# A two-block transformer on one core: block 1's norms leave their inputs undivided and multiply every accumulator by the inverse root

## The reference

```python
def rms_norm(x, g):
    xf = x.astype(jnp.float32)
    y = xf * lax.rsqrt(jnp.mean(xf * xf, axis=-1, keepdims=True) + EPS)
    return (y * g.astype(jnp.float32)).astype(x.dtype)

for l in range(DEPTH):                      # DEPTH = 2
    h = rms_norm(x, attn_norm_g[l])
    proj = h @ w_in[l]                      # 28 tiles of 128 outputs
    rq, rk, rv, rg, dq, dk, dv = jnp.split(proj, split_at, axis=-1)
    ...                                     # retention, gated by silu(rg); differential attention
    x = x + jnp.concatenate([ret, da], axis=-1) @ w_out[l]
    h = rms_norm(x, ffn_norm_g[l])
    x = x + (jax.nn.silu(h @ w_gate[l]) * (h @ w_up[l])) @ w_down[l]
```

## Time and profile before

| what | value |
|---|---|
| runs | 3076.81, 3080.22, 3081.91 us (median 3080.22) |
| the profiled execution | 3072.54 us, of which its span 3070.8 |
| granted TensorE clock, mean of the span | 0.988 of 2.4 GHz |
| busy: TensorE, VectorE, ScalarE, GpSimd | 97%, 52%, 37%, 34% |

### The profile page before, as it was taken

The page is one execution under the profiler, slowest core; times in us unless marked ns, Lnnn a source line. Parts: engine busy times, 40 slices in busy tenths (PEclk is TensorE's granted clock), DMA queues, the critical chain, the costliest instruction groups (busy, mean ns, idle before and its releaser), DMA issues.

```text
span 3070.8 us, 46525 instructions
## 1 busy us (share of the span) xinstructions
PE 2980.6 (97%) x16904; PEld 2394.7 (78%) x16904; DVE 1592.3 (52%) x2527; ACT 1144.7 (37%) x1735; POOL 1053.4 (34%) x458
## 2 busy tenths in 40 slices
PE   8999999999999999999999999999999899999999
PEld 6866787887857788877886788888888667878887
DVE  5357654556357544554316746541552347567372
ACT  4264441223274542232227733321232327543232
POOL 3433444443433444442220033222223330244443
PEclk9999999999999999999999999999999999999999
DMA  4421343433411343431121111121221120122223
GB/s 165 139 105 37 128 148 126 146 131 105 168 55 56 129 143 131 145 122 48 55 65 39 49 49 55 61 70 54 67 67 64 55 63 2 38 86 95 91 97 101
DMA packets 78028, 272.74 MB, mean 89 GB/s; under 512 B 8160, under 2 KB 15328, under 8 KB 77792
## 3 DMA queue, kind: packets, MB, share of 16 engines
q1 hardware_dynamic: 76256, 267.09, 26.6%
q10 hardware_dynamic: 1664, 4.18, 0.4%
HBM read 269.14 MB, written 2.10 MB: 88 GB/s over the span
## 4 chain that ended last, share of the span: by engine, by line
PE 57%; issue 26%; POOL 8%; DVE 5%; ACT 2%; POOLq 0%; DMA 0%; ACTq 0%; DVEq 0%
PE ps L653 43%; POOL w_lo L552 7%; PE ps L691 4%; PE ps L1038 1%; PE ps L731 1%; PE ps L1020 1%; PE ps L773 1%; DVE s_s L2042 1%; PE ps L881 1%; PE ps L870 1%; DVE s_s L2032 1%; PE ps L905 1%; PE ps L862 1%; DVE h_lo L1671 1%; PE ps L894 1%
## 5 line engine op out<-in xcount | busy, mean ns | idle before, releaser
L552 POOL TENSOR_TENSOR w_lo<-w_raw,w_hi 128x1024 fp32r<-128x1024 f32 (+1 forms) x364 | 945.2, 2597 | 1521.9 <-ACT w_hi L1156 1521.9
L653 PE MATMUL ps<-h_hi,w_hi 128*128 128x512 f32 (+1 forms) x2832 | 953.8, 371 | 4.6 <-DVE proj L1702 2.3
L653 PE MATMUL ps<-h_lo,w_hi 128*128 128x512 f32 (+1 forms) x2832 | 945.3, 368 | 0.0
L653 PE MATMUL ps<-h_hi,w_lo 128*128 128x512 f32 (+1 forms) x2832 | 945.2, 368 | 0.0
L1156 ACT ACTIVATE w_hi<-w_raw 128x1024 fp32r<-128x1024 f32 (+1 forms) x364 | 406.3, 1116 | 1346.7 <-PE ps L653 1225.5
L653 PEld LDWEIGHTS ps<-h_hi,w_hi 128*128 128x128 f32 x2832 | 490.6, 188 | 111.5 <-issue 12.7
L653 PEld LDWEIGHTS ps<-h_hi,w_lo 128*128 128x128 f32 x2832 | 490.2, 188 | 90.9
L653 PEld LDWEIGHTS ps<-h_lo,w_hi 128*128 128x128 f32 x2832 | 490.5, 188 | 88.6
L1816 DVE TENSOR_SCALAR conv_y<-u_pad,small 128x770 f32<-128x770 f32 (+1 forms) x88 | 176.3, 2004 | 192.2 <-ACT u_pad L1338 192.0
L1769 DVE SCALAR_TENSOR_TENSOR xT<-ps,mod,xT 128x512 f32 (+1 forms) x72 | 45.4, 659 | 306.7 <-PE ps L653 260.0
L1604 DVE CUSTOM_DVE_ANT_0 mod_junk<-mod_w,silu_c 128x1024 f32<-128x1024 f32 x96 | 140.7, 1465 | 118.7 <-DMA mod_w<-w_mod_dram 116.8
(11 more groups left out here) (213 smaller groups left out, 3702.6 us busy)
## 6 DMA issues: line engine op xcount, KB each, us to landing
mod_w<-w_mod_dram SPq DMA_DIRECT2D x96, 512.0 KB, 3.5
w_raw<-w_gu_dram SPq DMA_DIRECT2D x88, 512.0 KB, 3.3
w_raw<-w_down_dram SPq DMA_DIRECT2D x64, 704.0 KB, 4.0
w_raw<-w_up_dram SPq DMA_DIRECT2D x88, 512.0 KB, 3.3
w_raw<-w_in_dram SPq DMA_DIRECT2D x56, 512.0 KB, 3.4
w_raw<-na_qkv_dram SPq DMA_DIRECT2D x24, 512.0 KB, 3.3
w_raw<-w_out_dram SPq DMA_DIRECT2D x16, 512.0 KB, 3.4
n_bias<-rpb_dram SPq DMA_DIRECT2D x24, 256.0 KB, 3.0
```

What stands on the lines that cost most here:

```text
L552: pool.tensor_tensor(w_lo[par][:, 0:cols], w_raw[par][:, 0:cols], w_hi[par][:, 0:cols].bitcast(F32), ALU.subtract).then_inc(w_lo_ready, 1)
L653: last = pe.matmul(acc[par][:, to:to + n], w[par][:, k * P:k * P + P], r[:, k, frm:frm + n], start=begin, stop=end)
```

## The change

Block 1's norms are of a new kind, `late`. Its inputs are not divided by the root: `h_hi` is ScalarE's copy of `xT` times the gain (a column of `small`), and `h_lo` is VectorE's `xT * gain - h_hi`, for all 8 tiles (GpSimd makes none). The root is worked out while the first pair behind the norm runs: `pack_norm` stands in `fresh_pair` after its fourth step (after the tenth at the start of the kernel), `spread_norm` after the eleventh (fourteenth), a step being three matmuls. `fresh_pair` now runs the first unit whole and then the second (`alternate(8)`). VectorE copies the spread inverse roots into a tile in SBUF, `rb` [128, 512], and every accumulator of w_in and of gate and up is multiplied by it on VectorE:

- the 16 plain units and the 4 of the gate's silu per layer, which ScalarE copied before (L1273), are now VectorE's (`take_proj`); the silu is then ScalarE's, in place in SBUF
- the normed units were VectorE's copy (L1702) and are its product now
- in `glu` VectorE makes `glu_g = acc[0] * rb`, ScalarE `silu(glu_g)` in place, VectorE `glu_g * rb`, and `glu_a = acc[1] * glu_g` as before. The modulation stands between the first and the second of these; before it stood ahead of all

At the end of a `resid` of block 1, ScalarE's work is written out (`late_end`): h_hi 0, the last square, h_hi 1 and 2, w_hi of the second unit, h_hi 3 to 7, the root.

At the start of the kernel SP loads 32 columns of gains first; the first weights no longer wait for a part of x, the second unit's wait for the second quarter and `mod_w` for the last; ScalarE makes h_hi and w_hi as x comes and squares behind them; the set-up of small things, `condition` (the silu of c), and the first modulation come later.

Block 2's norms stay as they were.

```diff
-POOL_TILES = {"norm": (2, 4, 6), "mix": (0, 2, 5, 3, 6), "fin2": (0, 2, 4, 6)}
+POOL_TILES = {"late": (), "norm": (2, 4, 6), "mix": (0, 2, 5, 3, 6), "fin2": (0, 2, 4, 6)}
...
     def norm(block, layer, which, T):
-        add("norm", block=block, layer=layer, which=which, T=T)
+        add("late" if block == 1 else "norm", block=block, layer=layer, which=which, T=T)
...
         def _(sp):
-            sp.wait_ge(x_in[2], 16)
+            sp.dma_start(small[:, 0:GAINS], d["small"][:, 0:GAINS]).then_inc(gains_in, 16)
...
                         if not first:
                             sp.wait_ge(w_lo_ready, i * 2 + (u0 + par - 1))
+                        elif par:
+                            sp.wait_ge(x_in[1], 16)
...
                         if not first:
                             sp.wait_ge(mod_step, i * 2 + u0)
+                        else:
+                            sp.wait_ge(x_in[3], 16)
...
-                for par, k in LATE_LAST if hidden else alternate(6 if ph["T"] == S else 3):
+                order = LATE_LAST if hidden else alternate(KT if late else 6 if ph["T"] == S else 3)
+                for step, (par, k) in enumerate(order):
...
+                    if late and step == (9 if first else 3):
+                        pack_norm(ph["fresh"])
+                    if late and step == (13 if first else 10):
+                        spread_norm(ph["fresh"])
...
+                act.activation(n_sq[1][:, 0:S], xT[:, KT - 1, 0:S], ACT.Square).then_inc(n_sq_ready, 1)
+                hi_late(ph, 1)
+                hi_late(ph, 2)
+                split(1)
+                for k in range(3, KT):
+                    hi_late(ph, k)
+                root(ph)
+
+            def beginning(ph):
+
+                act.wait_ge(gains_in, 16)
+                for q in range(4):
+                    act.wait_ge(x_in[q], 16)
+                    hi_late(ph, 2 * q)
+                    hi_late(ph, 2 * q + 1)
+                    if q in (0, 2):
+                        hi_part(q // 2, 16, KT)
+                act.dma_start(lam_vec[:], d["lam"]).then_inc(loaded, 16)
+                act.dma_start(silu_c[:], d["c"]).then_inc(loaded, 16)
+                act.activation(stats[:, 20:21], eps1[:], ACT.Sqrt).then_inc(table_in, 1)
+                for k in range(KT):
+                    if k >= 2:
+                        act.wait_ge(n_added, k)
+                    act.activation(n_sq[k % 2][:, 0:S], xT[:, k, 0:S], ACT.Square).then_inc(n_sq_ready, 1)
+                root(ph)
...
+            def late(ph):
+
+                n0 = ph["norm0"]
...
+                def lo(k):
+                    dve.wait_ge(h_hi_ready, KT * ph["h0"] + k + 1)
+                    dve.scalar_tensor_tensor(out=h_lo[:, k, 0:S], in0=xT[:, k, 0:S],
+                                             scalar=col("g_" + ph["which"], KT * ph["layer"] + k),
+                                             in1=h_hi[:, k, 0:S].bitcast(F32), op0=ALU.mult, op1=ALU.subtract
+                                             ).then_inc(h_dve, 1)
...
+                for k in range(KT):
+                    lo(k)
+                    if k == 5 and n0:
+                        invert()
...
+                dve.wait_ge(n_cast, ph["chunk0"] + len(chunks(S)))
+                dve.tensor_copy(halves(row(rb[:])), spread_out(S)).then_inc(n_rb, 1)
...
+                def take(i, par):
+                    dve.wait_ge(mm_done, i * 2 + (ph["unit0"] + par + 1))
+                    dve.tensor_tensor(proj1[:, bass.ds(i * 2 + (ph["tile0"] + par), 1), :], row(acc[par][:, 0:S]), row(rb[:]),
+                                      ALU.mult).then_inc(acc_free, 1)
...
                 with dve.Fori(0, FH) as f:
+                    dve.wait_ge(mm_done, f * 2 + (ph["unit0"] + 1))
+                    dve.wait_ge(a_lo_ready, BEGUN + f + n0)
+                    dve.tensor_tensor(glu_g[:], acc[0][:, 0:S], rb[:], ALU.mult).then_inc(acc_free, 1)
                     modulation(f, ph["unit0"])
-                    dve.wait_ge(acc_free, f * 2 + (ph["unit0"] + 1))
+                    dve.wait_ge(glu_silu, f + (n0 + 1))
+                    dve.tensor_tensor(glu_g[:], glu_g[:], rb[:], ALU.mult).then_inc(glu_scaled, 1)
                     dve.wait_ge(mm_done, f * 2 + (ph["unit0"] + 2))
-                    dve.wait_ge(a_lo_ready, BEGUN + f + n0)
+                    dve.wait_ge(glu_scaled, f + (n0 + 1))
                     dve.tensor_tensor(glu_a[:], acc[1][:, 0:S], glu_g[:], ALU.mult).then_inc(acc_free, 1)
```

148 lines of the change are left out of this document (94 added, 54 removed).

## The result

The changed kernel takes 3086.91 us (median of 20 runs, 3080.98 to 3094.08) against 3079.29 us for the kernel before (median of 20). The ratio is 1.0027, with a 95% interval of 1.0019 to 1.0035, so it is slower by some 8 us. I had forecast 3.4 us faster: the sign is wrong. The measured median lies close to the 3087.8 us of rival 3, but by coincidence. That rival has the clock fall at all three norms and nothing gained at the start; what happened is mostly something else.

A forecast was written before the change was run, and what follows sets the result against it. TensorE, busy 97%, was taken as the bound. Gains of 12.1 us less 7.2 (gate/up loop) and 1.5 (clock) left 3.4 us; the profiled 3072.5 becomes 3069.1, plus 7.7 to the median gives 3076.8, range 3068 to 3087.

The forecast's parts named there:

- rival 3: Norms and start: clock falls again at all three norms, nothing gained at the start; 7.6 us slower, 3087.8; chance 0.15.
- Part 1: Norms ahead of the two gate/up stages: next pair starts 17.5 us after the last matmul's start; gains 3.7 and 3.3 us.
- Part 2: Norm ahead of layer 1's projections: TensorE gets the first accumulator 18.75 us after the last matmul's start; gain 1.6 us.
- Part 4: Gate/up loop: VectorE's second dot product holds up w_lo in first halves, 0.40 us a pair, 7.2 us lost; second halves nothing.
- rival 1: Gate/up loop hides its new work, so no pair is longer; 3069.6; chance 0.18.
- rival 2: Gate/up loop: VectorE reaches the second dot product late but still before w_lo; 0.86 us a pair, 3085.1; chance 0.10.
- rival 4: Norms: first pair is faster because h_lo 3 gets through ahead of w_lo; 2 us more at three norms, 3070.8; chance 0.07.
- Part 5: Block 1's projections and mix: VectorE's added accumulators and possible w_lo waits are covered, mix at most 0.3 us later; costed at nothing.
- Part 3: Start of the kernel: second pair starts at 32.2 instead of 35.71; gain 3.5 us, from 0 to 6 possible.
- The clock: First unit of three norms: 1.5 us lost to a lower TensorE clock.

The follow-up runs named there:

- split_last: Changed kernel with w_hi of the second unit moved behind h_hi 7 and the root, and the reciprocal behind h_lo 7; ratio to the kernel before 1.0007.

## Why the prediction was wrong, point by point

**What was right.** *Part 1*: the next pair at L+17.5 was forecast for two norms; measured 17.86, and 19.26 at the one where the clock fell. *Part 2*: 18.75 forecast, 20.04 measured with the clock down for 3.4 us; in the kernel with SP's other order, whose norms are the same, it is 18.54 without. *Part 4*: 0.40 us a pair and 7.2 in all were forecast, 0.43 and 7.7 measured, with w_lo, dot product and TensorE within 0.1 us of the times in the text, and nothing inside the second halves. Rivals 1, 2 and 4 fell with that. Here too the Trainium skill's rule of the one that comes later and fully blocks ("SBUF — State Buffer", Who interferes with whom) is borne out: behind a w_lo h_lo 3 took 2.36 us in place of 0.75, and the dot product 3.29 in place of 1.22.

**The step that failed first: Part 5, "I cost both at nothing".** The projections were looked at for VectorE's and GpSimd's time alone, and that did have cover. What I left out is who waits for the modulation's end. The text said that w_lo may wait for a dot product; it did not ask when the dot product itself, behind w_lo, ends, and what SP has queued behind it. The modulation starts behind the first accumulator and its dot product is held for 2 us more, so `mod_w` is loaded later, and the strips and the next weights behind it. For the plain pairs the claim held; at the gate's units, where the strips come in, it cost 3.5 us.

**The same omission in Part 4.** In the second halves I counted "w_lo comes at D+1.25, waits for the first dot product, and is done at D+4.3", which is right, and stopped there. The second dot product then ended at D+5.3, and the larger weights of the stage behind came late: 3.0 us in two exits. For the gate's units and for the exits alike, two experiments that each remove one link (the order on SP, the order on VectorE) remove the term, which is what shows the chain. That a held dot product does not always lead to a wait is shown by the plain pairs and by the kernel before with a late modulation.

**Part 3, the start.** Forecast: second pair at 32.2, 3.5 us gained. w_lo was indeed done at 32.44, but TensorE waited for the accumulator, which was queued behind the set-up and held up by that same w_lo: 34.05. Then the third pair's weights stood behind `mod_w` (40.13 in place of 35.12). 0.9 us lost, 4.4 off: in this profile the largest miss of any term. Four profiles have this start unaltered. Against before, the end of unit 8 comes 1.0 us later in the changed kernel and 0.1 earlier in the one with the modulation ahead in the projections. In the other two (gate/up modulation ahead, `split_last`) it comes 1.9 and 2.4 earlier. In these quick ones the clock stays up while the inverse roots are worked out, and the set-up is done before w_lo begins. The windows of the changed kernel and of the one with the gate/up modulation ahead, 22 to 28 us:

```profile
22.00:28.00 6.00, 5.39 (x62) 4.18 (x62) 1.02 (x2) 4.90 (x6) 0.00 (x0) 0.72 0.01 3
```

```profile
22.00:28.00 6.00, 5.11 (x77) 4.13 (x78) 1.29 (x3) 5.10 (x6) 0.00 (x0) 1.00 0.01 3
```

So the order was worth about 2 us where the clock did not fall in that stretch, and nothing where it fell; my 3.5 was too much in both cases.

**The clock.** 1.5 us were allowed. At the norms the fall is worth 1.4 or 1.5 us each where it comes (17.86 against 19.26, 18.54 against 20.04), and it came at two of the three, 2.9 us. I had said that in attention the clock stays up; it did not in the mix, twice, 3.4 us. So rival 3's mechanism was in part at work, in part at places that it did not name.

**The sum again**, forecast and measured in the first profiles: start -3.5 and +0.9; norms -7.1 (clock allowed for) and -5.3; first halves +7.2 and +7.7; gate's units 0 and +3.5; exits 0 and +3.0; mix 0 and +3.4. Block 1 together: -3.4 and +13.1. Against the second profile of before, block 1 is 10.7 us longer and block 2 is 1.3 shorter; together 9.4, near the timed 8. The falls of the clock in the mix come in some profiles and not in others, so a single profile, this one with two of them, does not give their share of the timed difference.

## What to carry to other kernels

When a piece of side work is moved, ask for its end as well as for its start. List what every queue, the DMA queue above all, has behind the semaphore that it raises, and check its slack at the places with the largest load (a change of shape, extra transfers), not in the middle of a loop. Where two engines exclude each other, as VectorE and GpSimd did here (w_lo 2.94 us in place of 2.40, the dot product 3.29 in place of 1.22), both directions count: whoever is pushed back passes the delay on to its own followers. And take a second profile of the kernel before, before a difference of 5 us between two traces is explained.
